# Two transformer blocks with expert choice: the router on raw feature blocks, GpSimd sums behind the experts, and context rows of two expert pairs in one tile

## The reference

```python
def expert_choice_ffn(h, w_router, w_g, w_u, w_d):
    B, n, D = h.shape
    cap = CAPACITY_FACTOR * n // N_EXPERTS          # 64 of 512 rows, 32 of 256
    logits = jnp.einsum('bnd,de->ben', h, w_router, preferred_element_type=jnp.float32)
    aff = jax.nn.softmax(logits, axis=1)
    gate, idx = lax.top_k(aff, cap)
    xs = h[bi, idx]
    a = jnp.einsum('becd,edf->becf', xs, w_g)
    u = jnp.einsum('becd,edf->becf', xs, w_u)
    y = jnp.einsum('becf,efd->becd', jax.nn.silu(a) * u, w_d)
    return jnp.zeros_like(h).at[bi, idx].add(y * gate[..., None].astype(y.dtype))

# in a layer, for the latent rows x and (layer 0 only) the context rows xc:
x = x + gt1 * latent_mixer(...)                      # ends with merged @ w_out
h2 = modulate(rmsnorm(x, g_ffn[l]), sh2, sc2)        # rmsnorm(x) * (1 + sc2) + sh2
x = x + gt2 * expert_choice_ffn(h2, w_router[l], w_e_gate[l], w_e_up[l], w_e_down[l])
```

## Time and profile before

| engine | busy us | share of the span |
|---|---|---|
| TensorE matmul (PE) | 3233.3 | 93% |
| TensorE weight load (PEld) | 2182.4 | 63% |
| VectorE (DVE) | 1442.8 | 41% |
| ScalarE (ACT) | 1002.0 | 29% |
| GpSimd (POOL) | 226.2 | 6% |

### The profile page before, as it was taken

How to read it: one execution, slowest core, us unless ns; L and a number is a source line. 1 busy time by engine, 2 the same in 40 slices (tenths; PEclk the granted TensorE clock), 3 DMA queues, 4 the chain that set the end, 5 groups by cost and what they waited for, 6 DMA issues and landing times.

```text
span 3483.8 us, 47130 instructions
## 1 busy us (share of the span) xinstructions
PE 3233.3 (93%) x20626; PEld 2182.4 (63%) x20630; DVE 1442.8 (41%) x2136; ACT 1002.0 (29%) x1566; POOL 226.2 (6%) x142
## 2 busy tenths in 40 slices
PE   6998999999799999999999997988879999989998
PEld 4886678887334344377668873332338766858886
DVE  3477655656301111156665542111135454453333
ACT  3624542223100100055443231000022354342223
POOL 0100000112100000001000210000002010120000
PEclk9999999999899999999999998999999999999999
DMA  8241013333799998734005539999973111323321
GB/s 217 53 130 43 1 55 103 109 109 123 269 397 367 392 350 344 260 50 131 25 1 157 165 133 395 420 421 421 421 278 97 35 49 43 91 67 97 97 97 67
DMA packets 395852, 616.95 MB, mean 177 GB/s; under 512 B 99234, under 2 KB 288896, under 8 KB 370944
## 3 DMA queue, kind: packets, MB, share of 16 engines
q1 hardware_dynamic: 388304, 596.50, 48.9%
q0 software_dynamic: 4384, 15.73, 1.3%
q10 hardware_dynamic: 2960, 1.72, 0.2%
HBM read 606.55 MB, written 7.34 MB: 176 GB/s over the span
## 4 chain that ended last, share of the span: by engine, by line
PE 80%; DMA 9%; DVE 6%; ACT 3%; issue 1%; POOL 0%; ACTq 0%; SPq 0%; DVEq 0%
PE ps L612 32%; PE ps L1876 6%; PE ps L2260 5%; PE ps L1134 4%; DMA ring<-in_w_e_up 4%; PE ps L1223 3%; PE ps L1912 3%; PE ps L1879 3%; PE ps L664 3%; DMA ring<-in_w_e_down 3%; PE ps L1184 3%; PE ps L1398 3%; PE ps L1871 2%; PE ps L633 2%; PE ps L1917 2%; PE ps L1908 2%
## 5 line engine op out<-in xcount | busy, mean ns | idle before, releaser
L612 PE MATMUL ps<-xh,wh 128*128 128x512 f32 x1912 | 638.8, 372 | 22.1 <-DVE xl L2106 11.7
L612 PE MATMUL ps<-xl,wh 128*128 128x512 f32 x1912 | 628.3, 367 | 0.0
L612 PE MATMUL ps<-xh,wl 128*128 128x512 f32 x1912 | 627.7, 366 | 0.0
L585 DVE TENSOR_TENSOR wl<-ring,wh 128x1024 fp32r<-128x1024 f32 (+1 forms) x259 | 318.6, 1230 | 296.6 <-ACT wh L576 295.9
L576 ACT ACTIVATE wh<-ring 128x1024 fp32r<-128x1024 f32 (+1 forms) x259 | 272.0, 1050 | 424.2 <-PE ps L612 168.1
L612 PEld LDWEIGHTS ps<-xh,wh 128*128 128x128 f32 x1912 | 329.3, 188 | 99.1 <-issue 20.8
L612 PEld LDWEIGHTS ps<-xl,wh 128*128 128x128 f32 x1912 | 330.3, 189 | 60.2 <-issue 0.5
L612 PEld LDWEIGHTS ps<-xh,wl 128*128 128x128 f32 x1912 | 328.1, 188 | 61.5
L1876 PE MATMUL ps<-ring,arena 128*32 128x512 f32 x1344 | 177.2, 599 | 0.9 <-ACT arena L1631 0.9
L1871 PE MATMUL ps<-ring,arena 128*64 128x512 f32 x704 | 163.1, 605 | 12.7 <-DMA ring<-in_w_e_up 8.1
L735 DVE SCALAR_TENSOR_TENSOR tmp<-ring,cs,tmp 128x512 f32<-128x512 f32 x224 | 167.4, 796 | 1.9
(11 more groups left out here) (281 smaller groups left out, 4517.6 us busy)
## 6 DMA issues: line engine op xcount, KB each, us to landing
ring<-in_w_e_gate SPq DMA_DIRECT2D x87, 1024.0 KB, 14.3
ring<-in_w_e_up SPq DMA_DIRECT2D x85, 1024.0 KB, 14.3
ring<-in_w_e_down SPq DMA_DIRECT2D x85, 1024.0 KB, 15.5
ring<-in_w_in SPq DMA_DIRECT2D x112, 512.0 KB, 4.1
ring<-in_w_ada SPq DMA_DIRECT2D x96, 512.0 KB, 4.4
arena<-in_w_e_up SPq DMA_DIRECT2D x43, 1024.0 KB, 11.8
arena<-in_w_e_down SPq DMA_DIRECT2D x43, 1024.0 KB, 14.7
arena<-in_w_e_gate SPq DMA_DIRECT2D x41, 1024.0 KB, 14.2
```

The source lines that it names most:

```text
L585: e.tensor_tensor(in_heads(X, u, m.WL[:, o:o + many]), heads_of(X, u, halves.aps[s], many), in_heads(X, u, m.WH[:, o:o + many].bitcast(F32 ...
L612: i = e.matmul(ps[0:M, a:b], w[:, k, 0:M], h[:, k, a:b], start=k == 0 and p == 0, stop=k == 7 and p == 2)
```

## The change

Three things change.

1. **The router works on raw blocks.** `RW` is router weight times gain, made by VectorE before the output projection. `pe_router` multiplies it with raw `XT`: blocks 0 to 3 behind output projection 5, blocks 4 to 7 behind the norm's sums, with one PSUM tile held in between. VectorE multiplies the result with `rst` instead of ScalarE's copy. The shift's part of the logits comes from small matmuls with a broadcast shift column, into the same PSUM tile as the fold. `HT` is gone: rows are turned from raw `XT`, scaled by `rst` in ScalarE's copy (`RC`, a column for each row chunk, made by small matmuls), written and gathered so, and gain and shift come with the eviction of the gathered rows, one block (in layer 0 one block and side) for each instruction. `pe_inner` waits for each block by itself. The chunks 0 and 1 are turned before the softmax is.
2. **Sums on GpSimd.** In the last combine of each layer the squares of blocks 1 to 4 (layer 0) or 1 to 3 (layer 1) are added by GpSimd; TensorE sums the next block, the total and the rest behind the combine.
3. **Context rows of two pairs in one tile.** The pairs of a combine write opposite halves of one `YC` tile, `GC` is made to match, and a combine needs two context matmuls a block; the clearing of the halves goes.

The diff, cut to its core:

```diff
+        RW = AR(R2 + 3072, 272)
+        RC = sm[:, 40:46]
+        RS1 = sm[:, 48:64]
...
+        def act_square_tail(e, stage, k, many, src, T, bufs, total, seen=lambda t: t):
+            if k > 2:
+                e.wait_ge(*(l_na.at(stage, k - 2) if k - 2 < many else p_n.at(stage, k - 2)))
+            dst = bufs[(k - 1) % 2] if k else total
+            e.activation(seen(dst[:, 0:T]), src, ACT.Square).then_inc(*n_sq.up(stage, k))
+
+        def pe_squares_tail(e, stage, many, T, bufs, total):
...
+            e.wait_ge(*n_sq.at(stage, many))
+            add(bufs[(many - 1) % 2], first=True).then_inc(*p_n.up(stage, many))
+            e.wait_ge(*l_na.at(stage, many - 1))
+            add(total)
+            for k in range(many + 1, KD):
+                e.wait_ge(*n_sq.at(stage, k))
+                add(bufs[(k - 1) % 2], last=k == KD - 1).then_inc(*p_n.up(stage, k))
...
+                if d == 5:
+                    pe_router(e, l, range(4))
...
+            for k in blocks:
+                for w, (a, b) in enumerate(segs(T)):
+                    o = 128 * w + 16 * k
+                    i = e.matmul(ps[32 * (k % 4):32 * (k % 4) + 32, a:b], RW[:, o:o + 32], XT[:, k, a:b],
+                                 start=k < 4, stop=k > 3, skip_group_check=True)
...
+            for w in range(many):
+                e.tensor_tensor(RW[:, 128 * w:128 * w + 128].rearrange("p (k e) -> p k e", e=16), wrv[:, l],
+                                A1v[:, l, 1, :, w:w + 1].broadcast_to([128, 8, 16]), ALU.mult).then_inc(
...
+            pe_router(e, l, range(4, KD))
+            rows(0)
+            lg, when = bank.take((st, "lg"), r_dve.at(st, "af"))
...
+            e.wait_ge(*n_rs.at(f"f{l}"))
             for c in range(ntc):
+                i = e.matmul(lg[:, 512 + c:513 + c], rst[:, 128 * c:128 * c + 128], ident[:, 0:1], start=c == 0, stop=True, skip_group_check=True)
...
-                e.activation(XS0[:, n % 4], tile.rearrange("p (k c) -> p k c", k=8)[:, :, 0:96], ACT.Copy).then_inc(*c_xs.up(st, n, half))
+            for k in range(4 * half, 4 * half + 4) if l else range(KD):
...
+                for w, (a, b) in enumerate(((0, 64), (64, 96))):
+                    e.activation(XS0[:, n % 4, k, a:b], tile[:, 128 * k + a:128 * k + b], ACT.Identity, bias=mcol(0, 3, k, w),
+                                 scale=A1v[:, 0, 1, k, w:w + 1]).then_inc(*c_xs.up(st, n, *((k,) if w else (k, "x"))))
...
-            for k in range(KD):
-                for w, (a, b) in enumerate(segs(T)):
-                    e.scalar_tensor_tensor(out=HT[:, k, a:b], in0=XT[:, k, a:b], scalar=A1v[:, l, 1, k, w:w + 1], in1=rst[:, a:b],
-                                           op0=ALU.mult, op1=ALU.mult).then_inc(*r_dve.up(st, "h", k, w))
+            e.wait_ge(*p_rt.at(st, "lgp"))
+            e.tensor_tensor(L_[1][:, 0:T], bank.of[st, "lgp"][:, 0:T], rst[:, 0:T], ALU.mult).then_inc(*r_dve.up(st, "lgp"))
...
-                for n, q in enumerate(pairs if c is not None else []):
-                    for j in (0, 1):
-                        i = e.matmul(c, YC[q % 2][j][:, 128 * k:128 * k + 128], MO[0].GC[:, q, :], start=n == 0 and j == 0,
-                                     stop=q == p and j == 1)
+                for j in (0, 1) if c is not None else ():
+                    i = e.matmul(c, YC[p // 2 % 2][j][:, 128 * k:128 * k + 128], MO[0].GC[:, 2 * (p // 2) + k // 4, :], start=j == 0,
+                                 stop=j == 1)
...
+        SUMMED = (5, 4)
...
+            for k in range(1, SUMMED[l]):
+                pool_square(e, f"n{l + 1}", k, T0 - NC_ * l, norm_bufs(l), norm_total(l))
```

More of the change, by code:

```diff
@@ L793, in pool_square, with add @@
             e.tensor_tensor(total[:, 0:T], total[:, 0:T], bufs[(k - 1) % 2][:, 0:T], ALU.add).then_inc(*l_na.up(stage, k))
+        def act_square_tail(e, stage, k, many, src, T, bufs, total, seen=lambda t: t):
[4 more added lines that the diff above has]
+        def pe_squares_tail(e, stage, many, T, bufs, total):
+            ps = bank.of["norm", stage]
+            def add(src, first=False, last=False):
+                for a, b in segs(T):
+                    i = e.matmul(ps[:, a:b], ones[:, :], src[:, a:b], start=first, stop=last)
+                return i
+            e.wait_ge(*n_sq.at(stage, many))
[5 more added lines that the diff above has]
+                add(bufs[(k - 1) % 2], last=k == KD - 1).then_inc(*p_n.up(stage, k))
         def pe_norm_take(e, stage):
@@ L1534, in pe_choice, with rows @@
             m = ME[l]
-            ps, when = bank.take((st, "lgp"), r_act.at(st, "lgp"))
+            def rows(c):
+                ps, when = bank.take((st, "h2", c), r_act.at(st, "h2", c))
+                for w in when:
+                    e.wait_ge(*w)
+                for k in range(KD):
+                    i = e.transpose(ps[:, k * 128:(k + 1) * 128], XT[:, k, c * 128:(c + 1) * 128], ident)
+                i.then_inc(*p_rt.up(st, "h2", c))
+            pe_router(e, l, range(4, KD))
+            rows(0)
@@ L1545, in pe_choice @@
-            i.then_inc(*p_rt.up(st, "lgp"))
-            ps, when = bank.take((st, "lg"), r_dve.at(st, "af"))
-            for w in when:
-                e.wait_ge(*w)
-            e.wait_ge(*r_act.at(st, "lgp"))
-            for c in range(ntc):
-                i = e.matmul(ps[:, 16 * c:16 * c + 16], L_[1][:, 128 * c:128 * c + 128], K("fold")[:, 0:16], start=c == 0, stop=True, skip_group_check=True)
+                for a, b, cap, c0, c1 in sides:
+                    e.matmul(lg[:, 16 * c0:16 * c1].rearrange("p (c e) -> p c e", e=16), modv[:, l, 24 + k, c0 // 4:c0 // 4 + 1].broadcast_to([128, 128]),
+                             wrv[:, l, k].unsqueeze(1).broadcast_to([128, c1 - c0, 16]), start=k == 0 and c0 == 0, stop=False,
+                             skip_group_check=True)
@@ new lines, in pe_choice @@
+            e.wait_ge(*n_rs.at(f"f{l}"))
+            for c in range(ntc):
+                i = e.matmul(lg[:, 512 + c:513 + c], rst[:, 128 * c:128 * c + 128], ident[:, 0:1], start=c == 0, stop=True, skip_group_check=True)
+            for n, of in enumerate((A1v[:, 1, 1, :, 0], modv[:, 1, 24:32, 0]) if l else ()):
+                for j in (0, 1):
+                    for h in (0, 1):
+                        o = 520 + 8 * n + j
+                        i = e.matmul(lg[64 * h:64 * h + 64, o:o + 7:2], ident[:, j:128:2], of[:, h:8:2], start=False, stop=True,
+                                     skip_group_check=True)
@@ L1552, in pe_choice @@
+            i.then_inc(*p_rt.up(st, "rc"))
+            e.wait_ge(*r_dve.at(st, "lgp"))
+            for c in range(ntc):
+                i = e.matmul(lg[:, 16 * c:16 * c + 16], L_[1][:, 128 * c:128 * c + 128], K("fold")[:, 0:16], start=False, stop=True, skip_group_check=True)
             i.then_inc(*p_rt.up(st, "lg"))
+            rows(1)
             ps, when = bank.take((st, "E"), r_dve.at(st, "E"))
@@ L1562, in pe_choice @@
             i.then_inc(*p_rt.up(st, "E"))
-            for c in range(ntc):
-                ps, when = bank.take((st, "h2", c), r_act.at(st, "h2", c))
-                for w in when:
-                    e.wait_ge(*w)
-                for k in range(KD):
-                    i = e.transpose(ps[:, k * 128:(k + 1) * 128], HT[:, k, c * 128:(c + 1) * 128], ident)
-                i.then_inc(*p_rt.up(st, "h2", c))
+            for c in range(2, ntc):
+                rows(c)
             ps, when = bank.take((st, "ix"), r_dve.at(st, "pick"))
@@ L1760, in back_tile, with ctx_pair @@
             return t[:, 0:512], t[:, 512:768]
+        def ctx_pair(batch_, half, rows):
+            return 2 * batch_ + (half ^ rows)
+        ctx_rows = lambda p, half: slice(64 * (half ^ p % 2), 64 * (half ^ p % 2) + 64)
         def dve_gates(e, l):
```

115 lines of the change are left out of this document (61 added, 54 removed).

## The result

The changed kernel took 3465.2 us (median of 4 runs, 3464.5 to 3467.0) beside 3485.9 for the kernel before (4 runs, 3484.0 to 3487.0): ratio 0.994, 95% interval 0.9928 to 0.9952, 20.7 us less. The profiled execution took 3464.6, with a span of 3462.6, 21.2 less than before. The forecast was 3467.8. Its terms did not all hold: one gave less than half of what it promised, and two effects that the sum doesn't have are together about as large as what it missed.

The account below looks back on a forecast made before the run. TensorE was taken to bound layer 0's expert stage and the weight stream layer 1's. The terms summed to 18.0 us, so 3485.8 - 18.0 = 3467.8, with a range of 3460 to 3478.

Parts of the forecast that it names:

- (a): Router blocks 0 to 3 inside the output projection: costs 2.0 us in layer 0 and 1.2 in layer 1.
- (b): Layer 0's expert choice: logits 9.8 us behind the norm's sums instead of 16.4, a gain of 6.6.
- (c): Evictions of the gathered rows in 16 pieces, 0.30 us each in layer 0: gains 0.2 us once.
- (d): Three combines inside layer 0's expert stage, with two context matmuls fewer a block: gain 1.9 us each, 5.7 in all.
- (e): Layer 0's last combine and the next norm, with GpSimd adding squares: gains 4.5 us.
- (f): Layer 1's choice: row chunks written earlier, so the weight stream doesn't run dry; gains 4.0 us.
- (g): Layer 1's last combine, with three of GpSimd's sums: gains 0.2 us.
- rival B: TensorE at 1.2 GHz in layer 0's choice and (e)'s sums: 5 off (b), 5.2 off (e), 3478 us; chance 0.14.
- my line: Time of an eviction piece on ScalarE: 0.26 us + 0.72 ns a column, so 0.30 a piece, 4.7 an expert.
- Rival D: Layer 0's evictions hold TensorE: at 1.0 us a piece each of 15 experts waits 2.5, 3506 us; chance 0.05.
- Rival C: Layer 1 gives nothing and narrow matmuls don't overlap: (f) is 0, (a) and (b) lose 2 each, 3475.8; chance 0.20.
- the last test that I named: Sign for (f) in layer 1's choice: no window under 350 GB/s between 2082 and 2120.

Follow-up runs that it names:

- e8_choice: The changed kernel with router blocks 0 to 3 moved from the output projection to the choice, in both layers: 3463.6 us, ratio 0.9938.
- e6_wide: The changed kernel with VectorE adding a block's 512-column part first and the context part behind it, each with its own signal: 3462.2 us, ratio 0.9931.
- e3_sums: The kernel before with GpSimd's sums behind the experts and nothing else of the change: 3480.7 us, ratio 0.9987.
- e7_rowslate: The changed kernel with layer 1's four row chunks turned, evicted and written behind the assembling of E, as before the change: 3467.5 us, ratio 0.9949.
- e2_pairs: The kernel before with the context rows of two pairs in one tile and nothing else of the change: 3476.9 us, ratio 0.9976.
- e4_router: The kernel before with the router part of the change alone: 3478.0 us, ratio 0.9978.
- e1_wr272: The changed kernel with the router weights' tile kept at 272 columns, 16 of them unused: 3469.7 us, ratio 0.9958.
- e11_cols8: The changed kernel with layer 0's gathered rows evicted in pieces of 8 columns, 96 an expert: 3618.9 us, ratio 1.0383.

## Why the prediction was right

Its sum was 18.0; the span fell by 21.2. By its terms, from the first two profiled executions:

| Term | Predicted | Measured | Where |
|---|---|---|---|
| (a) layer 0, 1 | -2.0, -1.2 | -1.3, -1.2 | how much later the next projection comes |
| (b) | 6.6 | 7.8, again 6.4 | inverse root to first expert matmul, 46.8 before, then 38.9 and 40.3 |
| (c) | 0.2 | 0 | wait of the first matmul 0.9 as before |
| (d) | 5.7 | 2.4 | three combines, 11.7 to 10.9 |
| (e) | 4.5 | 4.7 | last `y` eviction to inverse root, 27.3 to 22.6 |
| (f) | 4.0 | 2.4 to 3.5 | SyncE's gate; last weight less sums |
| (g) | 0.2 | 0.9 | last combine to table load |
| outside | 0 | 4.4 to 5.5 | pace 1.6, half clock 1.6, rest scattered |

**(a)** The 1.7 for eight narrow matmuls was a choice between 1.3 and 5.4, and the lower bound was right: a block's two matmuls on one group overlap with those of the next group (1.44 for eight, 1.29 side by side). In layer 0 the 0.3 for two switches of form didn't come: the fold in front of them is narrow as well, so the switch was paid already. In layer 1 no fold stands there, and the switches show: 0.09 going in and 0.10 coming out, with 1.0 for the four matmuls, 1.2 as predicted. That agrees with the Trainium skill's rule that I weighed ("TensorEngine Tiling (Array Packing)", Key Properties).

**(b)** The mechanism held: TensorE alone from sums to logits, 8.6 us in the first trace, small matmuls at 0.22 instead of 0.25. But rival B's condition came true more often than not. In all ten traces of kernels with the router part the granted clock falls to 0.50 in this choice, though TensorE isn't idle from the sums on. In three, the first trace among them, that is 9 us behind the sums and the logits are there at 8.6; in seven it is 6 to 8 us behind them, and the logits come at 9.2 to 10.7 (`e8_choice`: 12.4). So the first trace is a lucky one, and the repeated one, 10.3, is like most. By my own sign of being wrong ("if the small matmuls run at 0.50") the reading of the clock failed there. Its price is small: 1.4 up to the first expert matmul in the repeated execution, not the rival's 5. With this choice (b) is worth 5.8 to 7.8 in all.

**(c)** A piece took 0.29 against my line's 0.30, and the combines don't wait for it. The estimate by the Trainium skill's prices ("ScalarE: Activation LUTs", What ACT_TABLE_LOAD costs), 0.32, is further off. Rival D falls with that; the runs at 16 and 8 columns confirm its condition, but its price was too high, for it charged every expert. Rival C falls with (a) and (f).

**(d)** This is the step that failed: "VectorE [...] has about 1.16 and just keeps up. So nearly all of it stays: 1.9 each." VectorE does have 1.16, and keeps up at it once the order is right (`e6_wide`). I compared two throughputs and left out the trip: with two tiles, matmuls into one wait for the adds out of it, 1.33 a block. Before the change TensorE went without a gap at 1.45 a block, so the trip didn't show. It left 0.8 of 1.9 a combine, 2.4 of 5.7 in all.

**(e)** Right, for the reason given: TensorE waits 0.95 for ScalarE at the first sum and ScalarE for GpSimd at squares 3 to 5; the end is 18.5 behind the first combine matmul, where 19 was said. Rival B's other half didn't come: the sums run at 1.00, and the half clock lies in the first blocks of this combine. `e3_sums` gives the sums 4.3 of it. GpSimd took 1.95 a sum.

**(f)** The logits came 5.7 earlier behind the sums (6.1 us), more than the 4.3 counted, and it didn't matter, as said: the stream sets the time. But here a second step failed, "so the three transfers are issued before the stream runs dry". The writes are issued 11 to 8 us earlier behind the sums and the last one lands only 2.4 earlier, since it takes 14.2 us instead of 8.4. The three transfers follow it 0.8 us before the last weight ahead of them lands, and the windows from 2086 to 2090 show a dip (columns as in the earlier trace rows), against the last test that I named. My lower bound, "writes end only with the weights ahead of them", isn't what happens either: three of the four land well before. The term isn't worth 0, since before the change the last write came 4.5 us behind the last weight (issued at 2099.68, landed at 2108.1, the weight at 2103.6). The Trainium skill has an ordering at this place ("DMA: Bandwidth & Descriptors", Queues, rings and completion order: a transfer's signal lands only after every earlier write of that DMA engine, across its queues). Whether it has a part in the 14.2 us no run here shows.

```profile
2086.00:2088.00 2.00, 0.60 (x8) 0.53 (x8) 1.00 (x4) 0.00 (x0) 0.00 (x0) 0.50 0.80 334
2088.00:2090.00 2.00, 0.00 (x0) 0.00 (x0) 0.00 (x0) 0.00 (x0) 1.18 (x2) 0.50 0.65 147
```

Over all traces, not only the first two: the last weight of layer 1 lands 495.7 to 497.6 us behind the sums in the four kernels with the old choice and 492.7 to 495.0 in the nine with the new one (`e7_rowslate` left out). The means differ by 2.7, so 2.4 to 2.7 is nearer to what (f) is worth than the 3.5 of the first two traces.

**(g)** The 0.9 can't be told from scatter. From the last combine to the table load it is 12.1 to 14.5 us in the kernels without GpSimd's sums and 12.1 to 12.6 in those with them, and `e2_pairs`, which leaves these sums as they were, has 12.1.

**Outside the sum.** (d) and (f) were short by 4 to 5 together. (a), (b) and (g) gave 2 to 3 back, and the rest, 4.4 to 5.5, came from places that the change doesn't touch. So the number came out close partly by luck: two terms too large, against effects that the sum doesn't have.

## What to carry to other kernels

Where two engines hand tiles to each other, compare three times: each engine's work per tile, and the round trip through a tile divided by the number of tiles. When the slower engine is relieved, the trip can become the longest of the three. Here it was shortened by emptying and signalling first the part that the other side wants first, with neither engine doing less. And a small write issued behind a full stream of weights shares that stream's rate: it took 9 to 14 us here where it took 6 to 8 near the stream's end, so issuing it 8 to 11 us earlier brought 2.4.

## What the runs showed that I had not expected

**Half clock behind the same idle time, or not.** Behind the gate and up matmuls of layer 0's last expert TensorE has one stretch with little work, 3.5 us with six transposes in it, alike in all traces. Behind it the kernel before runs its first 16 matmuls at 0.50 in 3.33 us, and so do `e3_sums` (3.13), `e4_router`, `e1_wr272` (3.03) and `e11_cols8`, in whole or for the most part; in the changed kernel, its repetition and the seven others the same take 1.71 at 1.00. Kernel before, then changed:

```profile
1451.00:1452.00 1.00, 0.88 (x8) 0.29 (x12) 0.01 (x1) 0.00 (x0) 0.00 (x0) 0.50 0.00 0
```

```profile
1440.00:1441.00 1.00, 1.00 (x12) 0.45 (x16) 0.00 (x0) 0.00 (x0) 0.00 (x0) 1.00 0.00 0
```

All three kernels without the context pairs have it, and two of eleven with them. `e1_wr272` does the same work in this stage as the changed kernel and has it, so no part of the change rules it out; what decides is open. The same holds for the choice, where the clock falls earlier in some traces than in others of the same program. It is worth 1.6 us each time, as much as some terms of the sum. The executions of one kernel spread by 2 to 5 us here, so single microseconds are read from stretches of a trace, not from totals.

**The projections' pace** is the other: 8.32 or 8.48 for 48 matmuls, with the clock at 1.00 in both, and fixed for each program.
